# First two weight slots of each sublayer: one 512-column operand, and the second slot's low part made on GpSimd

## What is computed

```python
def rms_norm(x, g):
    y = x * rsqrt(mean(x * x, axis=-1, keepdims=True) + 1e-6)
    return y * g

# every sublayer, with its own weights and its own pair of gains
h = rms_norm(x, ng[pre])
x = x + weight * rms_norm(sublayer(h), ng[post])

# ffn: D_FF = 2816
g, u = h @ w_gate, h @ w_up
y = (silu(g) * u) @ w_down
# ret, mla, stick: h @ w_in, a retention or attention on it, and @ w_o
```

## Time and profile before

| what | value |
|---|---|
| median of 3 runs | 1942.08 us (1941.95 to 1942.27) |
| the profiled execution, its own time | 1942.17 us |
| its span from the first to the last instruction | 1940.2 us |
| granted TensorE clock over the span | 0.999 |
| busy: PE, PEld | 1914.6 us (99%), 1688.8 us (87%) |
| busy: DVE, ACT, POOL | 1285.5 us (66%), 1031.2 us (53%), 183.3 us (9%) |
| chain that ended last | PE 96%, ACT 1%, DVE 1%, issue 1% |

### The profile page before, as it was taken

The page is one execution under the profiler, slowest core; times in us unless marked ns, Lnnn a source line. Parts: engine busy times, 40 slices in busy tenths (PEclk is TensorE's granted clock), DMA queues, the critical chain, the costliest instruction groups (busy, mean ns, idle before and its releaser), DMA issues.

```text
span 1940.2 us, 29023 instructions
## 1 busy us (share of the span) xinstructions
PE 1914.6 (99%) x11272; PEld 1688.8 (87%) x11272; DVE 1285.5 (66%) x1335; ACT 1031.2 (53%) x1190; POOL 183.3 (9%) x160
## 2 busy tenths in 40 slices
PE   7999999999999999999999999999999999999998
PEld 7888989888888888888898889888888888988887
DVE  4766756666676667666676666766667666667665
ACT  5544664544554457644464446654455445665443
POOL 2600213100010001100010001210001000301000
PEclk9999999999999999999999999999999999999999
DMA  8555554555565553465556556366566556545553
GB/s 304 196 195 195 172 166 141 195 195 187 181 200 190 185 174 136 149 206 193 183 186 196 188 186 211 110 196 195 193 193 198 174 193 196 196 130 185 185 186 106
DMA packets 262263, 356.25 MB, mean 184 GB/s; under 512 B 9008, under 2 KB 230576, under 8 KB 262192
## 3 DMA queue, kind: packets, MB, share of 16 engines
q1 hardware_dynamic: 258592, 342.15, 54.0%
q0 software_dynamic: 3600, 13.11, 1.8%
HBM read 354.19 MB, written 1.05 MB: 183 GB/s over the span
## 4 chain that ended last, share of the span: by engine, by line
PE 96%; ACT 1%; DVE 1%; issue 1%; DMA 0%; POOL 0%; SPq 0%; DVEq 0%; POOLq 0%; ACTq 0%
PE down L514 29%; PE gate_banks L437 15%; PE up_banks L437 14%; PE gate_banks L441 8%; PE up_banks L441 7%; PE up_banks L420 3%; PE up_banks L422 3%; PE up_banks L421 3%; PE up_banks L482 3%; PE up_banks L473 3%; PE up_banks L474 3%; PE gate_banks L554 1%; PE gate_banks L584 1%; PE up_banks L451 0%; PE up_banks L453 0%
## 5 line engine op out<-in xcount | busy, mean ns | idle before, releaser
L1323 DVE TENSOR_TENSOR w_lo<-raw,w_hi 128x2048 fp32r<-128x2048 f32 (+1 forms) x311 | 710.5, 2287 | 277.2 <-ACT w_hi L942 276.9
L942 ACT ACTIVATE w_hi<-raw 128x2048 fp32r<-128x2048 f32 x322 | 613.5, 1905 | 204.2 <-PE down L514 178.7
L437 PE MATMUL gate_banks<-h_both,w_hi 128*128 128x512 f32 x1280 | 321.1, 393 | 0.0
L437 PE MATMUL up_banks<-h_both,w_hi 128*128 128x512 f32 x1152 | 287.5, 392 | 0.0
L514 PE MATMUL down<-w_hi,m_hi 128*128 128x512 f32 x832 | 268.2, 394 | 0.0
L437 PEld LDWEIGHTS gate_banks<-h_both,w_hi 128*128 128x128 f32 x1280 | 230.9, 189 | 41.4
L514 PE MATMUL down<-w_lo,m_hi 128*128 128x512 f32 x832 | 265.0, 390 | 0.0
L514 PE MATMUL down<-w_hi,m_lo 128*128 128x512 f32 x832 | 264.8, 390 | 0.0
L437 PEld LDWEIGHTS up_banks<-h_both,w_hi 128*128 128x128 f32 x1152 | 211.3, 189 | 40.4
L441 PEld LDWEIGHTS gate_banks<-h_both,w_lo 128*128 128x128 f32 x1280 | 174.7, 191 | 12.5
L514 PEld LDWEIGHTS down<-w_hi,m_lo 128*128 128x128 f32 x832 | 156.4, 188 | 33.2
(11 more groups left out here) (231 smaller groups left out, 2328.3 us busy)
## 6 DMA issues: line engine op xcount, KB each, us to landing
raw<-in_ffn_w_gu SPq DMA_DIRECT2D x88, 1024.0 KB, 5.1
raw<-in_ffn_w_down SPq DMA_DIRECT2D x88, 1024.0 KB, 4.9
raw<-in_ffn_w_gate SPq DMA_DIRECT2D x44, 1024.0 KB, 5.3
raw<-in_ffn_w_up SPq DMA_DIRECT2D x44, 1024.0 KB, 5.3
raw<-in_w_in SPq DMA_DIRECT2D x20, 1024.0 KB, 5.6
raw<-in_ret_w_in SPq DMA_DIRECT2D x13, 1024.0 KB, 5.3
raw<-in_w_o SPq DMA_DIRECT2D x8, 1024.0 KB, 5.0
raw<-in_w_out SPq DMA_DIRECT2D x8, 1024.0 KB, 4.9
```

Of the source, the lines that this page charges most:

```text
L437: mm(both, w_hi[:, r, c:c + P], h_both[:, k, :, :].rearrange("p a b -> p (a b)"), start=(k == 0), stop=(k == KD - 1), skip_group_check=True)
L942: act_fn(w_hi[:, r, 0:width], raw[:, r, 0:width], ACT.Copy).then_inc(hi_ready, 1)
L1323: v.tensor_tensor(w_lo[:, r, 0:width], raw[:, r, 0:width], w_hi[:, r, 0:width].bitcast(f32), ALU.subtract).then_inc(lo_ready, 1)
```

## The change

- In `first_slots`, matmuls of t = 0 and t = 1 take the columns of slot b and slot b + 1 as one moving operand of 2 x 256 = 512 columns (`high_both`, `low_both`). `bank0` now holds t = 0 of both slots and `bank1` t = 1 of both. Both low parts have to be there before the first `low_both`. At the very start (p = 0) t = 0 stays in single slots.
- The turns of t = 1 are made in two groups of four, the first in front of the first half of `low_both`, the second in the middle of it.
- GpSimd makes both halves of the low part of slot b + 1: the first where it was, the second behind `post_root` of t = 1. DVE's `low_second_half` is gone.
- DVE does `post_add` and `pre_scale` of t = 1 half by half in turn, not two and two.
- `slot_done` rises by 2 at the end of both slots. Readers wait for `first_half` for t = 0 (`first_out`, and silu and product of an ffn by halves).

```diff
+            def high_both(n, bank, p, t, hi, lo):
+
+                pe.wait_ge(hi_ready, n + 2)
+                o, ts = bank[:, :].rearrange("p (a b) -> p a b", a=2), slice(t * P, (t + 1) * P)
+                for k in range(KD):
+                    if k % 4 == 0:
+                        pe.wait_ge(h_lo_done, 4 * p + 2 * t + k // 4 + 1)
+                    mm(o, hi[:, k, ts], both_slots(w_hi, n, k), start=(k == 0), stop=False)
+                    mm(o, lo[:, k, ts], both_slots(w_hi, n, k), start=False, stop=False)
+
+            def low_both(n, bank, t, hi, ks=range(KD)):
+
+                take(n + 1)
+                o, ts = bank[:, :].rearrange("p (a b) -> p a b", a=2), slice(t * P, (t + 1) * P)
+                for k in ks:
+                    last = mm(o, hi[:, k, ts], both_slots(w_lo, n, k), start=False, stop=(k == KD - 1))
+                return last
...
-                (n0, bank_a), (n1, bank_b) = parts
-                high_passes(n0, bank_a, p, 0, hi, lo)
-                low_pass(n0, bank_a, 0, hi)
...
+                    high_both(n, banks[0], p, 0, hi, lo)
+                    turn_half(p, 1, 0)
+                    low_both(n, banks[0], 0, hi, range(KD // 2))
+                    turn_half(p, 1, 1)
+                    low_both(n, banks[0], 0, hi, range(KD // 2, KD)).then_inc(first_half, 1)
                 second()
-                high_passes(n1, bank_b, p, 0, hi, lo)
-                turn(p, 1)
-                low_pass(n1, bank_b, 0, hi)
-                for n, bank in parts:
-                    high_passes(n, bank, p, 1, hi, lo)
-                    low_pass(n, bank, 1, hi).then_inc(slot_done, 1)
+                high_both(n, banks[1], p, 1, hi, lo)
+                low_both(n, banks[1], 1, hi).then_inc(slot_done, 2)
...
-                        rows_out(b, u, [(c_nat[:, :, 0:QR], 0, QR)])
+                        first_out(0, b, u + 1, [(c_nat[:, 0, 0:QR], 0, 0, QR), (c_nat[:, 0, QR:QR + KVR], 1, 0, KVR), (kr[:, 0, :], 1, KVR, KVR + ROPE)])
                         high(b + 3, width=2 * HEADS_M * QKW)
-                        rows_out(b + 1, u, [(c_nat[:, :, QR:QR + KVR], 0, KVR), (kr, KVR, KVR + ROPE)])
+                        first_out(1, b, u + 1, [(c_nat[:, 1, 0:QR], 0, 0, QR), (c_nat[:, 1, QR:QR + KVR], 1, 0, KVR), (kr[:, 1, :], 1, KVR, KVR + ROPE)])
...
                 post_gained(u, 1, 0)
                 post_gained(u, 1, 1)
-                post_add(u, 1)
-                pre_scale(u + 2, 1)
-                low_second_half(b + 1)
+                ve.wait_ge(post_rs, 2 * u + 2)
+                for c in range(2):
+                    post_add_half(u, 1, c)
+                    pre_scale_half(u + 2, 1, c)
                 pre_low(u + 2, 1)
+                ve.wait_ge(lo_ready, b + 2)
                 low(b + 2)
...
                 post_root(u, 0)
                 if u + 1 < U:
-                    low_first_half(u)
+                    low_half(u, 0)
                 post_root(u, 1)
+                if u + 1 < U:
+                    low_half(u, 1)
                 if u + 1 < U:
                     load_post_gain(u + 1)
                     pre_root(u + 2, 0)
```

More of the change, by code:

```diff
@@ L269, in build, with side_of @@
         U = len(SUBLAYERS)
-        U_OF = {first_slot[u + 1] + 1: u + 1 for u in range(U - 1)}
         ROWS_BEFORE = [sum(k != "mla" for k in SUBLAYERS[:u]) for u in range(U)]
+        def side_of(n, s):
+            return s if n % RING < (n + 1) % RING else 1 - s
         def wait(eng, s, value):
@@ L471, in high_passes @@
                     if k % 4 == 0:
                         pe.wait_ge(h_lo_done, 4 * p + 2 * t + k // 4 + 1)
[L473 to L479, removed]
+                    mm(o, hi[:, k, ts], w, start=(k == 0), stop=False)
@@ L480, in low_pass @@
+                    mm(o, lo[:, k, ts], w, start=False, stop=False)
+            def low_pass(n, s, bank, t, hi):
+                take(n + s)
+                o, ts = bank[:, side_of(n, s) * SC:(side_of(n, s) + 1) * SC], slice(t * P, (t + 1) * P)
                 for k in range(KD):
-                    c = k * SC
-                    last = mm(o, hi[:, k, ts], w_lo[:, n % RING, c:c + SC], start=False, stop=(k == KD - 1))
-                return last
-            def first_slots(p, parts, hi=h_hi, lo=h_lo, second=lambda: None):
+                    last = mm(o, hi[:, k, ts], w_lo[:, (n + s) % RING, k * SC:(k + 1) * SC], start=False, stop=(k == KD - 1))
+                return last
@@ L649, in _ @@
             pe.wait_ge(const_in, 16)
-            first_slots(0, [(n, next_bank()) for n in range(2)], m_hi, m_lo)
+            first_slots(0, 0, [next_bank() for t in range(T)], m_hi, m_lo)
             take(2)
@@ L700, in _ @@
                     mem = list(mem_heads(0, 0))
-                    first_slots(u + 1, [(b + j, next_bank()) for j in range(2)])
+                    first_slots(u + 1, b, [next_bank() for t in range(T)])
                     spread_scale(u)
@@ L1017, in copy_out, with first_out @@
                 evacs[0] += 1
+            def first_out(t, n, p, dsts):
+                sc.wait_ge(*((first_half, p + 1) if t == 0 else (slot_done, n + 2)))
+                if p:
+                    sc.wait_ge(pre_rs, 2 * p + t + 1)
+                bank = gemm_bank[evacs[0] % 2]
+                for dst, s, c0, c1 in dsts:
+                    at = side_of(n, s) * SC
+                    last = act_fn(dst, bank[:, at + c0:at + c1], ACT.Copy, scale=scale_of(t) if p else 1.0)
+                last.then_inc(evac, 1)
+                evacs[0] += 1
             def rows_out(n, u, dsts, func=ACT.Copy):
@@ L1073, in _ @@
                     pre_high(1, 0)
-                copy_out(n, (mv if n < 2 else mk_T)[:, n % 2, :, :])
+                if n < 2:
+                    first_out(n, 0, 0, [(mv[:, s, n, :], s, 0, SC) for s in range(2)])
+                else:
+                    copy_out(n, mk_T[:, n % 2, :, :])
                 high(n + 3)
@@ L1339, in pre_scale @@
                 for c in range(2):
[L1340 to L1347 removed]
+                    pre_scale_half(p, t, c)
             def diag(u):
```

106 lines of the change are left out of this document (61 added, 45 removed).

## The result

| kernel | median us | lowest to highest | ratio to before, 95% interval |
|---|---|---|---|
| before | 1942.01 | 1941.70 to 1942.27 (6 runs) | 1 |
| after | 1960.73 | 1960.15 to 1961.23 (6 runs) | 1.0097 [1.0087, 1.0107] |

What follows compares the result with a forecast made beforehand. PE, busy 99% of the span, was taken to bound the kernel. New waits less cheaper steps gave +14.9 us at eleven places, mla +0.9, the start -0.7: +15.1, so 1957 us, range 1945 to 1966.

Steps and rivals of the forecast that it cites:

- PE's matmuls: Places between sublayers: 512-column steps at 0.228 us replace pairs costing 0.240; a place falls from 12.73 to 11.98 us without waits.
- rival (d): Matmuls at the places: the two-piece operand costs 0.240 us a step, +7 us on any case; chance 0.08 of the forecast.
- The new wait: Turns of t = 1: GpSimd's second half blocks DVE's post_add, so PE waits 2.10 us; +1.35 a place, +14.9 for eleven.
- (b): DVE beside GpSimd's half: DVE is let in halfway, PE waits some 1.2 us, +0.5 a place, 1948 us; chance 0.11.
- (c): DVE beside GpSimd's half: no blocking, PE waits 0.3 us for the low part, -0.4 a place, 1938 us; chance 0.13.
- (a): GpSimd's half is served last, PE waits at the low part; 1969 us, or 1962 if before the last pre_scale; chance 0.16.
- The mla sublayer: PE's wait for c_nat: high(b + 3) of 1.16 us now comes ahead of the last copies; +0.9 us, once.
- The start: Start of the kernel (p = 1): no GpSimd half stands in the way, so the place gains its 0.7; -0.7 us.
- Cover behind the place: Behind each place: high(b + 3) and the low part start later, 4.2 to 4.7 us, covered by 5.6 or 5.8 of matmuls.

Runs made afterwards that it cites:

- experiment 9: Kernel after, but GpSimd fills the second half of the low part with zeros by memset, reading nothing, where it subtracted; 1933.41 us, 0.9957 of before.
- 10: Kernel after, with GpSimd's second piece cut to 256 columns and the other 768 columns of the low part left out; 1938.65 us, 0.9984 of before.
- Experiment 1: Kernel after, with DVE again making the second half of slot b + 1's low part behind its last pre_scale; 1961.41 us, 1.0099 of before.
- Experiment 4: Kernel after, but t = 0's low part in single slots, turns between them, low part shared and DVE's order as before; 1938.35 us, 0.9982 of before.
- Experiment 5: Kernel after, with eight superfluous 512-column matmuls (1.82 us) ahead of the first turns; 1956.81 us, 1.0076 of before.
- experiment 6: Kernel after, with GpSimd's second half held back until DVE's last pre_scale of t = 1 is done; 1986.1 us, 1.0225 of before.
- experiment 3: Kernel before, with only GpSimd making both halves of the low part; 256-column matmuls and old order kept; 1958.63 us, 1.0086 of before.
- experiment 7: Kernel after, with ACT's high(b + 3) in the mla sublayer behind the copies of both tiles instead of between them; 1960.92 us, 1.0094 of before.

## Why the prediction was right, and what it missed

**PE's matmuls: right.** The step of L499 and L500 is 0.228 us, the two-piece operand costs nothing (rival (d) falls), and the place without a block takes 11.99 us (experiment 9) where the sum had 11.98.

**The new wait: right in mechanism, place and size.** The order on GpSimd against DVE came out as written (356.30 against 356.37), `post_add` took 2.87 us where about 3 was named, and the turns stand 360.09 - 358.01 = 2.08 us behind the point at which PE was ready, where 2.10 was worked out. The places at which the clock holds cost 1.32 us more than before, and 1.35 was forecast. Experiments 9 and 10 show the mechanism itself: the instruction that reads two operands blocks, the memset that only writes doesn't, and the loser waits for the whole instruction. The Trainium skill (SBUF — State Buffer, Who interferes with whom) states it so, and L1425, the case that no row of before had, agrees (2.87 us beside the subtraction, 0.75 beside the memset). Rivals (b) and (c) are ruled out by the 2.87 us, and (a) by GpSimd's 2.39: it was served first. One reading that led there was loose: L1868 was called a reader of two operands from SBUF and has one tensor operand. And (a)'s 1969 is 1968 by its own terms (1942 + 26 + 0.2).

**What the argument had not seen.** It priced the block, and not the order of the work by itself. Experiment 1 shows that without it, and with DVE making the half, PE waits just as long at the low part. The new order asks for `xn` and for slot b + 1's low part 0.41 us apart (360.09 and 360.50), and DVE has four instructions and a half low part to make. Experiment 4 asks for both later, and gains.

**The clock: missed.** The sum priced a standstill at its length, and put what it does to the clock at nothing. In three of eleven places the granted clock also fell, 1.53 us each, 4.6 in all, where the profiled span exceeds the forecast by 4.0. Experiment 5 fills the standstill and gets 3.9 us back. This is the term that was left out, and the one that was priced too low in experiment 6. That the time stayed inside the range owes something to luck here: with a fall at all eleven places it would, by these 1.53 us, be an estimated 12 us more, about 1973.

**Small terms.** The mla sublayer cost 1.07 us, 0.9 forecast. The start gained 1.09, 0.7 forecast; by itself it varies by more than the 0.4 between them (its group of matmuls stands between 55.02 and 55.61 us in seven kernels with the same first part, and at 56.54 in experiment 1). The sum of what was mis-sized is -0.3 (the places), +0.2, -0.4 and +4.6: 4.1, and the rows' 19.1 against 15.1 is that, rounded.

**Cover behind the place.** Nothing else came late: the list of PE's waits has no new line beside the one of L583 but 0.3 us once at L499, at the start, where the forecast had it. So `high(b + 3)` is hidden, as forecast.

## What to carry over

Before an instruction is moved from one engine to another, look at what the other engines run in the stretch where it lands, and at whether both sides read SBUF; a GpSimd instruction released by the same event as DVE's critical one takes nearly its whole length from DVE (2.12 of 2.39 us here). When PE's steps are made cheaper or its operands joined, everything that it reads is needed earlier and together, so list for each operand when it is asked for and when it is ready. Price a standstill of PE at its length and, as a second case, with slower matmuls behind it (1.5 us for a fall here).

## What the runs showed of the hardware

- **The granted clock after a standstill.** PE stood for 1.3 us at 11 places (experiment 3) and the span's clock stayed at 1.000. It stood for 1.90 to 1.94 us at 11 places (the kernel after) and fell to the lower level at three, though the waits are alike. It stood for 3.2 us (experiment 6) and fell at ten; a place then cost 4.0 us more than before, against 1.7, and only 1.3 of the 2.3 between them are the longer wait. In experiment 7, with waits as long, it fell at three again, but one of them was another place. What tells the three from the other eight, and the one from the ten, stays open.
- **A blocked DVE instruction shows as a long one.** Nothing in PE's list of waits names GpSimd: `post_add` is charged 2.87 us as busy time. The only signs are a maximum four times the median at one line, and the other engine's row beside it.
- **GpSimd is as fast when it wins.** Its 1024 columns took 2.39 us beside a waiting DVE, and 2.41 beside one that reads PSUM.
